# A two-block transformer kernel: setup and first modulations in one phase, three more orders moved

## What is computed

```python
# first block
mod = jax.nn.silu(c) @ w_ada[l] + b_ada[l]            # 6 x 1024 modulations
shift1, scale1, gate1, shift2, scale2, gate2 = jnp.split(mod[:, None, :], 6, axis=-1)
h = x * (1.0 + scale1) + shift1                        # needs the first 2 x 1024 of mod
...
g_attn, g_ssd = jnp.split(jax.nn.sigmoid(g_logits), N_BRANCHES, axis=-1)
mixed = (g_attn * y_attn + g_ssd * y_ssd) @ w_out[l]
x = layer_norm(ALPHA * x + gate1 * mixed, ln1_g[l], ln1_b[l])
h2 = x * (1.0 + scale2) + shift2
# PEER, for each token block
act = jax.nn.gelu(jnp.einsum('thk,td->thk', expert_u[eidx], tb), approximate=False)
wts = (g * act.astype(jnp.float32)).astype(tb.dtype)
return jnp.einsum('thk,thkd->td', wts, expert_v[eidx])
...
# second block, layer 0: RWKV-7, 16 heads of width 64, a state S per head
y = _rwkv7_mix(h, ...)
```

## Time and profile before

| what | value |
|---|---|
| median of 3 runs | 4340.25 us (4338.29 to 4346.74) |
| the profiled execution | 4345.02 us |
| its span | 4343.3 us |
| PE busy | 4096.5 us, 94% of the span |
| DVE, ACT, POOL busy | 57%, 36%, 35% |
| granted clock, mean | 0.968 |

### The profile page before, as it was taken

The page is one execution under the profiler, slowest core; times in us unless marked ns, Lnnn a source line. Parts: engine busy times, 40 slices in busy tenths (PEclk is TensorE's granted clock), DMA queues, the critical chain, the costliest instruction groups (busy, mean ns, idle before and its releaser), DMA issues. The chain is left out here.

```text
span 4343.3 us, 65491 instructions
## 1 busy us (share of the span) xinstructions
PE 4096.5 (94%) x26058; PEld 3332.2 (77%) x26058; DVE 2490.0 (57%) x4398; ACT 1569.7 (36%) x2159; POOL 1514.2 (35%) x659
## 2 busy tenths in 40 slices
PE   4999997989999999999999999899989998998998
PEld 3777776868888888778888875688867886777887
DVE  5786765778886888457666435256535623433221
ACT  2555453233334444322222233344323223443222
POOL 2333332434443333344444422311124442313443
PEclk9999998999999999999999999899989999999999
DMA  4333326633334554566667622200014642212232
GB/s 150 104 100 100 98 94 207 205 99 126 128 128 160 186 179 174 181 231 232 228 233 236 197 84 78 60 3 3 3 43 171 210 128 75 78 44 78 97 95 90
DMA packets 235199, 555.65 MB, mean 128 GB/s; under 512 B 17336, under 2 KB 101944, under 8 KB 226016
## 3 DMA queue, kind: packets, MB, share of 16 engines
q1 hardware_dynamic: 231520, 527.39, 36.7%
q10 hardware_dynamic: 3456, 25.17, 1.7%
HBM read 472.71 MB, written 79.77 MB: 127 GB/s over the span
## 5 line engine op out<-in xcount | busy, mean ns | idle before, releaser
L1692 POOL TENSOR_TENSOR peer_wl<-peer_wf,peer_wh 128x1024 fp32r<-128x1024 f32 x272 | 704.9, 2592 | 956.1 <-ACT peer_wh L1705 956.0
L1705 ACT ACTIVATE peer_wh<-peer_wf 128x1024 fp32r<-128x1024 f32 x272 | 286.1, 1052 | 521.4 <-PE peer_y L1803 514.5
L2120 POOL TENSOR_TENSOR ff_wl<-ff_wf,ff_wh 128x1024 fp32r<-128x1024 f32 (+1 forms) x136 | 317.9, 2337 | 449.1 <-ACT ff_wh L2187 449.1
L1801 PE MATMUL peer_y<-peer_xh,peer_wh 128*128 128x512 f32 x1152 | 456.4, 396 | 9.2 <-DVE peer_xl L1906 7.4
L1803 PE MATMUL peer_y<-peer_xh,peer_wl 128*128 128x512 f32 x1152 | 449.6, 390 | 0.0
L1802 PE MATMUL peer_y<-peer_xl,peer_wh 128*128 128x512 f32 x1152 | 449.4, 390 | 0.0
L1832 PE MATMUL peer_y<-peer_twh,peer_wh 128*128 128x512 f32 x1024 | 405.5, 396 | 11.2 <-DVE peer_twl L1998 11.2
L1833 PE MATMUL peer_y<-peer_twl,peer_wh 128*128 128x512 f32 x1024 | 405.3, 396 | 0.0
L1834 PE MATMUL peer_y<-peer_twh,peer_wl 128*128 128x512 f32 x1024 | 405.2, 396 | 0.0
L629 POOL TENSOR_TENSOR br_wl<-br_wf,br_wh 128x1024 fp32r<-128x1024 f32 x80 | 197.1, 2463 | 392.9 <-ACT br_wh L833 392.9
L2187 ACT ACTIVATE ff_wh<-ff_wf 128x1024 fp32r<-128x1024 f32 (+1 forms) x136 | 140.7, 1035 | 519.5 <-PE ff_acc L2149 345.3
(11 more groups left out here) (597 smaller groups left out, 8823.7 us busy)
## 6 DMA issues: line engine op xcount, KB each, us to landing
peer_wf<-in_u SPq DMA_DIRECT2D x128, 512.0 KB, 3.6
peer_wf<-in_v SPq DMA_DIRECT2D x128, 512.0 KB, 3.8
ff_wf<-in_w_gu SPq DMA_DIRECT2D x88, 512.0 KB, 3.5
br_wf<-in_w_in SPq DMA_DIRECT2D x80, 512.0 KB, 3.6
acts<-peer_aout SPq DMA_DIRECT2D x128, 256.0 KB, 2.0
gates<-peer_gout SPq DMA_DIRECT2D x16, 2048.0 KB, 7.3
peer_gout<-gates SPq DMA_DIRECT2D x32, 1024.0 KB, 7.5
peer_gout<-acts SPq DMA_DIRECT2D x128, 256.0 KB, 5.4
```

The costliest lines, as they stand in the source:

```text
L1692: nc.gpsimd.tensor_tensor(wl[:, t % SLOTS], wf[:, t % 2], wh[:, t % SLOTS], ALU.subtract).then_inc(w_low, 1)
L1705: nc.scalar.activation(wh[:, t % SLOTS], wf[:, t % 2], ACT.Copy).then_inc(w_high, 1)
L1801: nc.tensor.matmul(out, wh[:, slot, k], xh[:, k], start=(k == 0), stop=False)
L2120: nc.gpsimd.tensor_tensor(wl[:, u % SLOTS, 0:n], wf[:, u % SLOTS, 0:n], wh[:, u % SLOTS, 0:n], ALU.subtract).then_inc(w_low, 1)
```

## The change

It has four parts, each in another phase.

1. ada_phase goes; setup_phase does its work. SP loads the vectors, then eight pieces of 1 MB (half a chunk each, in the order of chunks 0, 1, 3, 2), then x. ACT makes csil first. DVE sums chunks 0, 1 and 2, and makes its comparisons and masks between them. PE does chunk 3 without DVE, as 32 matmuls of the weights with a column of csil. DVE adds the bias from PSUM.
2. mix_phase: columns(h) three tiles behind DVE's sums in place of one (LAG), with four part buffers (PARTS); the running total shares the slot of stage 0.
3. peer_phase: SP loads the first gates and the first three experts' activations ahead of the last three stores, and ACT rounds the first weights ahead of the last eviction.
4. rwkv_heads_phase: other_factors is cut in four: kt stays, sq comes earlier (behind y5), bh and kh come behind the first state step of the next pair, rt behind its center.

```diff
@@ setup_phase, sync
-                sp.dma_start(C.X[:], io["x"]).then_inc(loaded, 16)
-                sp.dma_start(C.vec[:], io["vec"]).then_inc(loaded, 16)
+                sp.dma_start(C.vec[:], io["vec"]).then_inc(vec_loaded, 16)
+                for n in (0, 1, 2, 3, 6, 7, 4, 5):
+                    sp.dma_start(w[:, n], ada_piece(io, 0, n)).then_inc(piece_loaded[n], 16)
+                sp.dma_start(C.X[:], io["x"]).then_inc(x_loaded, 16)
+                sp.wait_ge(x_loaded, 16)
...
@@ setup_phase, vector
+                def chunk(c):
+                    for n in (2 * c, 2 * c + 1):
+                        dve.wait_ge(piece_loaded[n], 16)
+                        for k in range(KT // 2):
+                            at = KT // 2 * (n % 2) + k
+                            if at:
+                                dve.wait_ge(stepped, KT * c + at)
+                            ada_step(nc, part[:, c], part[:, c], w[:, n, k], C.csil[:, 0:8], at).then_inc(stepped, 1)
...
+                dve.wait_ge(silu_done, 1)
+                chunk(0)
+                dve.wait_ge(made, 1)
+                same_blocks(0, 4)
+                chunk(1)
+                same_blocks(4, 7)
...
+                chunk(2)
+                dve.wait_ge(summed, ADA_FIRST)
+                nc.vector.tensor_tensor(C.mod[:, 0:12], acc[:, 0:12], C.v("b_ada", 0, 12), ALU.add).then_inc(biased, 1)
+                nc.vector.tensor_tensor(C.mod[:, 12:16], direct[:, 0:4], C.v("b_ada", 12, 4), ALU.add).then_inc(biased, 1)
+                dve.wait_ge(biased, 2)
+                nc.vector.tensor_scalar(C.mod[:, 8:16], C.mod[:, 8:16], 1.0, None, ALU.add)
...
@@ setup_phase, tensor
+                for c in range(ADA_FIRST - 1):
+                    if c == ADA_FIRST - 2:
+                        pe.wait_ge(silu_done, 1)
+                        for n in range(4):
+                            for k in range(KT):
+                                if n == 0 and k % 4 == 0:
+                                    pe.wait_ge(piece_loaded[6 + k // 4], 16)
+                                last = nc.tensor.matmul(direct[:, n:n + 1], w[:, 6 + k // 4, k % 4, n * P:(n + 1) * P],
+                                                        C.csil[:, k:k + 1], start=(k == 0), stop=(k == KT - 1))
+                        last.then_inc(summed, 1)
+                    pe.wait_ge(stepped, KT * (c + 1))
+                    for n in range(4):
+                        last = nc.tensor.matmul(acc[:, 4 * c + n:4 * c + n + 1], part[:, c, n * P:(n + 1) * P],
+                                                C.ones[:, 0:1], start=True, stop=True)
+                    last.then_inc(summed, 1)
...
@@ first_block
-    ada_phase(nc, io, C)
...
@@ mix_phase
-    BANKS, SLOTS, STAGE, RING = 5, 2, 4, 3
+    BANKS, SLOTS, STAGE, RING, PARTS, LAG = 5, 2, 4, 3, 4, 3
-        total = ph.sb("total", [P, S])
+        total = stage[:, 0]
-                    ada_columns(nc, mods[:, 2 * h:2 * h + 2], part[:, h % 2], C).then_inc(summed, 1)
+                    ada_columns(nc, mods[:, 2 * h:2 * h + 2], part[:, h % PARTS], C).then_inc(summed, 1)
-                    for h in halves_of(t - 1):
+                    for h in halves_of(t - LAG):
+                    if h >= PARTS:
+                        dve.wait_ge(summed, h - PARTS + 1)
...
@@ peer_phase, sync and scalar
-                for r in range(2):
-                    sp.wait_ge(gates_stored[r], 16 * (BLOCKS // 2))
-                for e in range(A_RING - 1):
-                    load_weights(e)
+                    if t == SCORE_TILES + 1:
+                        for r in range(2):
+                            sp.wait_ge(gates_stored[r], 16 * (BLOCKS // 2))
+                        for e in range(A_RING - 1):
+                            load_weights(e)
...
+                def weight_high(e):
+                    act.wait_ge(weighted, e + 1)
+                    if e >= 2:
+                        act.wait_ge(projected, SCORE_TILES + e - 1)
+                    nc.scalar.activation(twh[:, e % 2], wts[:, e % 2], ACT.Copy).then_inc(wt_high, 1)
+
                 for t in range(SCORE_TILES + 1):
+                    if t == SCORE_TILES:
+                        weight_high(0)
...
@@ rwkv_heads_phase, vector
-                def other_factors(j):
+                def bonus_factors(j):
+                    stt(out=buf("sq", j), in0=r_of(j), scalar=C.v("r_k", j), in1=buf("k2", j), op0=ALU.mult,
+                        op1=ALU.mult).then_inc(rk_made, 1)
+
+                def reading_factors(j):
+                    dve.wait_ge(exps, 5 * j + 5)
+                    tt(buf("rt", j), r_of(j), buf("cum", j), ALU.mult).then_inc(rt_made, 1)
+
+                def key_factors(j):
                     tt(buf("kt", j), buf("k2", j), buf("sgw", j), ALU.mult).then_inc(kt_made, 1)
+
+                def end_factors(j):
                     tt(buf("bh", j), buf("ka", j), buf("dc", j), ALU.mult)
                     tt(buf("kh", j), buf("k2", j), buf("dc", j), ALU.mult).then_inc(bh_kh, 1)
-                    tt(buf("rt", j), r_of(j), buf("cum", j), ALU.mult).then_inc(rt_made, 1)
-                    stt(out=buf("sq", j), in0=r_of(j), scalar=C.v("r_k", j), in1=buf("k2", j), op0=ALU.mult,
-                        op1=ALU.mult).then_inc(rk_made, 1)
 
                 def first_state(j):
                     dve.wait_ge(g_ready, j + 1)
@@ -2986,7 +2986,9 @@
                 key_inverse(0)
                 unit_keys(0)
                 first_factors(0)
-                other_factors(0)
+                key_factors(0)
+                bonus_factors(0)
+                reading_factors(0)
                 for i in range(RW_PAIRS):
                     prv, nxt = i > 0, i + 1 < RW_PAIRS
                     if prv:
@@ -2994,6 +2996,7 @@
                     masked("at", i, "AT", strict64[:])
                     if prv:
                         next_state(i - 1, 1)
+                    end_factors(i)
                     link(tt(chunked(buf("y", i)), chunked(buf("AT", i)), wide(level64[:, 0]), ALU.mult))
                     tt(chunked(buf("y", i)), chunked(buf("y", i)), wide(ident64[:]), ALU.add).then_inc(y_first, 1)
                     masked("akt", i, "akt", strict64[:])
@@ -3004,6 +3007,8 @@
                         for c in range(3, CHUNKS - 1):
                             next_state(i - 1, c)
                         center(i - 1)
+                    if prv:
+                        reading_factors(i)
                     added("x1", i, "x")
                     added("y1", i, "y")
                     added("x2", i, "x")
@@ -3021,6 +3026,8 @@
                         weighted_keys(i + 1)
                     masked("arb", i, "arb", C.keep64[:])
                     added("y5", i, "y")
+                    if nxt:
+                        bonus_factors(i + 1)
                     if prv:
                         output(i - 1)
                     if nxt:
@@ -3030,7 +3037,7 @@
                         first_factors(i + 1)
                     kept(tt(buf("ht", i), read("ht", i), buf("rt", i), ALU.add), "ht", i)
                     if nxt:
-                        other_factors(i + 1)
+                        key_factors(i + 1)
                 last_pair = RW_PAIRS - 1
                 first_state(last_pair)
                 for c in range(1, CHUNKS - 1):
```

91 lines of the change are left out of this document (22 added, 69 removed).

## The result

| what | before | after |
|---|---|---|
| median | 4340.86 us (4338.29 to 4346.74, 4 runs) | 4294.60 us (4292.43 to 4295.40, 4 runs) |
| span of the profiled execution | 4343.3 us | 4293.7 us |
| granted clock, mean | 0.968 | 0.972 |

The ratio is 0.9893, with a 95% interval of 0.9881 to 0.9905: 46.3 us faster. The forecast was 4290 (4279 to 4304).

The account below looks back on a forecast made before the run. PE's waits were taken as the bound: first modulations, mixing sums, values' start and RWKV pair borders. Gains 17.4 + 1.6 + 13.5 + 17.5 = 50.0 us from the median 4340.25 gave 4290 us, range 4279 to 4304.

Parts of the forecast that it names:

- The start: Setup: DVE can begin its first modulation sum at 7.0 us, when the first 1 MB weight piece has landed.
- PE's direct path: Setup: PE's 32 one-column matmuls for chunk 3 take 14.9 us, ending 1.6 us later than DVE's chain.
- the middle: Setup: gain taken as 17.4 us, between 16.6 (PE ends last) and 18.2 (clock rises, DVE's chain decides).
- the next bound stands close behind: Mixing: without the sums' wait, PE waits for tile 9's low weights at 761.6 against 763.9, leaving 2.3 us, net 1.6.
- rival 4: Mixing: the phase keeps its clock since PE's idle times split, 5.2 us more gain, 4285 us; chance 12%.
- only the last bound counts: Mixing: PE idles before tile 9 in both cases, so only 763.9 - 761.6 = 2.3 us is won there.
- twl(1): Values' start: next item to be late, ready about 1842.5 plus up to 2 us against PE's need at 1844.7.
- Rival 3: Values' start: loads land after 1839 or the chain behind is late; 13.5 us not won, 4303.5 us; chance 4%.
- the new wait at the third step: Pair borders: PE reaches chain(3) at 2902.2, before akt mask and next_state(2) end at 2902.9; 0.7 us lost.
- The surcharge of 1.8 us: Pair borders: extra time of DVE ops beside POOL's two levels, counted once for both y ops, bh and kh.
- rival 1: Pair borders: the clock still falls, 1.7 us per border stay lost, 5.5 us less than forecast, 4296 us; chance 15%.
- rival 2: Pair borders: the DVE-POOL lock holds for whole instructions, chain(3) wait grows 0.7 us per border, 4295 us; chance 8%.

Follow-up runs that it names:

- part 2 alone: The kernel before with only the mixing-phase part (columns three tiles behind, four part buffers): 4338.47 us, ratio 0.9996.
- the five experiments that leave this phase as in after: The kernel after with edits only in setup or heads (one run twice): 4296.15, 4298.52, 4292.21, 4297.79 and 4298.18 us.
- parts 1, 2 and 3 alone: Three kernels, each the one before with only the setup, mixing or values part of the change: 4323.65, 4338.47 and 4327.57 us.
- The kernel with both further moves: After, with DVE's takes ahead of its sums in mixing, and rt and the next pair's weighted keys moved later in heads: 4278.36 us, ratio 0.9856.
- nd_busy: After with chunk 3 summed on DVE, plus PE's 32 one-column matmuls added back with result unused: 4297.79 us, ratio 0.9896.
- delay: After with six unread extra DVE copies before setup's last adds, shifting later phases by 1.6 us: 4298.52 us, ratio 0.9898.

## Why the prediction was right

**Part 1, 17.4 us predicted, 18.4 measured.** The start was 7.0 and came at 6.51; DVE's end 39.4, came at 38.9; PE's direct path 14.9 us, took 13.8. All three were on the safe side, by 0.5, 0.5 and 1.1 us. That PE, not DVE, ends last was right, but by 0.6 us and not 1.6. The row of four matmuls in 1.87 us, which I took as 0.47 each, holds the start of the group too: within 32 in a row one takes 0.43. I took the middle between a clock that stays low under this run and one that rises. The pace says that it stayed low. The same four matmuls of one column take 1.05 us in br at clock 1.00 (the row at 272.00 in the last section), and in a low stretch of br they take 1.76 us; in setup they take 1.85 to 1.87, before and after. Before, PE in br:

```profile
673.85 1.76 PE L738 MATMUL br_gacc<-ones,br_sqb 128*128 128x1 f32 x8 [0.78 <-ACT br_sqb L893]
...
674.00:676.00 2.00, 2.00 (x10) 2.00 (x11) 0.07 (x1) 0.57 (x2) 0.00 (x0) 0.50 0.00 0
```

So the case that came was the slow one, 16.6 us, and the safe sides of the other terms made it 18.4; the middle of 17.4 came close by luck.

**Part 2, 1.6 us predicted, 1.9 measured between the two profiles, but not to be told from nothing.** Four executions with the old order took 201.4, 200.3, 202.3 and 201.8 us in the phase, seven with the new one (after, part 2 alone, and the five experiments that leave this phase as in after) 199.5 to 203.1, on average 200.7: a gain of 0.8 us from an average of 201.5. The step "the next bound stands close behind" was right to the place: I named waits of 2.8 us before tile 6 and 3.5 before tile 9, and 2.67 and 4.12 came. The step that failed is the clock. I let both tiles run as slowly as before, where a low stretch of 6.9 us stands at each; in after these stretches are 3.4 us each. So half of what rival 4 named did happen, but not its 5.2 us: the wait for the sums (7.0 us) went and the clock gave back about 4 us over the phase, while the waits for low weights rose from 1.7 to 10.8 us and took most of both. That reasoning, "only the last bound counts", carried the forecast, not the size of its terms.

**Part 3, 13.5 us predicted, 13.6 measured.** Issue behind the store, 14.1 us ahead of PE's need (1808.32 to 1822.4; I had 14); landing 8.2 us after the issue, at 1816.47 (the upper one of my two estimates was 10.5); no wait at PE; the clock at 1.00. Of the small wait behind it that I allowed for (twl(1)) nothing shows in PE's rows. Rival 3 fell.

**Part 4, 17.5 us predicted, 16.8 measured.** From border to border it is 47.74 - 45.09 = 2.65 us, against 2.7 (seven of them made 18.5; that I took 17.5 had no reason in the sum). But the two halves of that sum were both off, and they offset each other. For the waits I counted 2.0 - 0.7 - 0.3 = 1.0 us; PE's idle time fell by 1.6. For the clock I counted 1.7; PE's busy time fell by 1.05 to 1.1. The small waits came lower than predicted: at-wait 0.45, came at 0.35; the new wait at the third step 0.7, came at 0.40; x1 0.3, came at 0.17; the copy wait 0.35, is gone. The surcharge of 1.8 us was counted once for four ops and measured 0.86 + 1.07 = 1.9 us, all on bh and kh, none on the y ops.

That the clock holds at the border was right, and rival 1 did not come. In the four traces with the old order (the kernel before and parts 1, 2 and 3 alone) a low stretch of 3.4 us begins within 1.4 us of the state copy at all seven borders; in the ten with the new order at none. What the forecast had at nothing is that low stretches come elsewhere in the pair: each of the ten traces has one to three, 31 to 33 us behind a border, where of the four old ones only the kernel before has one. After has two, and these two periods take 46.63 and 46.40 us instead of 45.09. No wait stands ahead of them; in all ten traces each of these low stretches begins within 2.5 us of two groups of eight matmul records with two columns each. After, PE, and the window behind:

```profile
2892.36 1.05 PE L2619 MATMUL rw_bank<-ones_bd,rw_x 128*128 128x2 f32 x8
2893.27 1.03 PE L2619 MATMUL rw_bank<-ones_bd,rw_sq 128*128 128x2 f32 x8
2894.23 1.97 PE L2591 MATMUL rw_bank<-rw_q,rw_y 64*64 64x64 f32 x32
...
2894.00:2898.00 4.00, 4.00 (x79) 3.98 (x80) 1.53 (x4) 0.70 (x3) 0.00 (x0) 0.57 0.00 0
```

On rival 2: the rule of the Trainium skill in "SBUF — State Buffer", section "Who interferes with whom", makes the port pair an exclusive lock for a whole instruction. The trace agrees: bh begins 0.27 us behind POOL's first level product and ends 0.54 us behind its end (2864.87), kh ends 0.54 us behind the end of the second (2866.55), and the ops behind both take 0.68. What did not come is the price that I worked out from it, two full POOL ops or 2.5 us. In these rows a DVE op that begins while POOL is at work has only the rest of that POOL op before it, so the two took 0.9 and 1.1 us more than alone, and the wait at the third step did not grow.

**The sum.** 50.0 predicted, 50.7 at the four places between the two profiles, 46.3 between the medians. Over all executions the places gave less than in that one pair: the chain averages 348.6 us in four executions with the old order and 332.6 in eight with the new one (16.0), scores and values 1650.3 against 1637.0 (13.3), mixing 0.8, setup 18.3: 48.4. The last 2 us are within the spread of the medians. I took the saving from the median with the reason that its stages do not differ between runs. For setup and values this is so (0.3 and 1.5 us of spread); for the mixing phase and the heads it is not (3.6 and 3.1 us in unchanged code). So the total of 50 is near the 46.3 (41 to 52 by its interval) partly because errors inside parts 1 and 4 offset each other.

## What to carry to other kernels

When a wait of the bounding engine is taken away, ask at once what that engine would wait for next: where it is a loop of other engines (here take, gate load, sources, low weights), the engine's own order is worth nothing, and the one line that shortens the loop was worth 10 us. Loads that depend on nothing late belong ahead of the last stores of the stage before, and products that a sequential chain doesn't read belong behind the step that it waits for. A sum that comes out right is checked term by term, here by idle and busy time of one period; and where the clock's record may not reach, the duration of the same shape elsewhere tells the rate. Judge a part of some tenths of a percent by its phase in several traces, since the total of this kernel moves by 10 us and more without any edit.

## What the runs showed of the hardware

The clock falls in steps of 3.4 us at half rate, and a wait of the same length in the same code is followed by one or not. PE in br, the wait and the window behind it, first before, then after:

```profile
272.00 1.05 PE L738 MATMUL br_gacc<-ones,br_sqb 128*128 128x1 f32 x8 [1.45 <-ACT br_sqb L893]
...
274.00:276.00 2.00, 2.00 (x10) 1.63 (x9) 0.18 (x1) 1.75 (x4) 0.00 (x0) 1.00 0.00 0
```

```profile
253.47 1.05 PE L725 MATMUL br_gacc<-ones,br_sqb 128*128 128x1 f32 x8 [1.45 <-ACT br_sqb L880]
...
256.00:258.00 2.00, 2.00 (x6) 1.57 (x5) 0.00 (x0) 1.82 (x3) 0.11 (x1) 0.50 0.14 55
```

br has eight waits of this kind (0.78 or 1.45 us, 8.2 us in all) in each execution. In after, all five low stretches ahead of the phase's end lie right behind one, two behind 1.45 us and three behind 0.78; the other executions had two to five such stretches. The kernel with both further moves, which has the same code up to there, has this wait too and clock 1.00 behind it:

```profile
254.99 1.05 PE L725 MATMUL br_gacc<-ones,br_sqb 128*128 128x1 f32 x8 [1.45 <-ACT br_sqb L880]
...
256.00:258.00 2.00, 2.00 (x10) 1.65 (x10) 0.18 (x1) 1.75 (x4) 0.00 (x0) 1.00 0.00 0
```

The wait at the borders of the pairs is another matter: 2.59 us, 1.83 at the first, it was followed by a fall at all seven borders in each of the four traces that have it. In setup PE kept the slow pace through 13.8 us of matmuls with one column, without a wait between them (64 records, one each 0.213 us; in br at clock 1.00 one each 0.11).

So unchanged phases move: br between 632.1 and 639.4 us, ff between 936.4 and 942.0 us, the kernel before between 4331.8 and 4353.0. By its rate a fall costs at most 1.7 us; where the periods of the heads can be compared, one costs 1.3 to 1.5 (46.40 and 46.63 against 45.09 after, 49.20 against 47.74 before). What decides which of br's short waits gets one is not settled: neither PE's activity before (nd_busy) nor a shift (delay) does it in a way that these runs can tell from chance.
